# Regrouping the attention matmuls of the second block by head, with the 16 meta keys in 16-row and 16-column tiles

## The chip, the cores and the metric

The kernel runs on one core of one Trainium2 chip. The metric is the device time of one execution in microseconds. The kernel before takes 3297.89 us, the median of three runs (3297.15 to 3299.16).

## The reference

Two blocks of two layers each follow one another. The first (`hybrid_layer`: differential and stick-breaking attention over 256 tokens, model width 2048) is not touched by the change. The second puts 16 meta tokens ahead of the 256 tokens and runs two layers that mix a convolution, a recurrence and this attention, with 16 query heads of size 64, 4 key heads, a window of 128 and one sink logit per head:

```
s_meta = einsum("bnqkgd,bmkd->bkgnqm", qb, km) * scale      # 16 meta keys
s_band = einsum("bnqkgd,bnjkd->bkgnqj", qb, k_band) * scale # own and previous block of 128
probs = softmax(concatenate([s_meta, where(valid, s_band, NEG_INF), sink_col], -1))
out_r = einsum(p_meta, vm) + einsum(p_band, v_band)
s_mm = where(causal, einsum("bqkgd,bmkd->bkgqm", qmg, km) * scale, NEG_INF)  # meta queries
```

The meta queries' own outputs are needed in the first of the two layers only, since the last layer's meta rows are dropped.

## The kernel before

Weights stream from memory in halves of 128x1024 words through a ring of four buffers `raw`. ScalarE rounds each to `w_hi`, VectorE writes the rest to `w_lo`, and TensorE makes three products per tile (hi by hi, lo by hi, hi by lo). In the second block these are lines L1808 to L1810, over all 272 tokens in layer 0 and over 256 in layer 1 (`FROM[l]` is 0, then 16).

Attention is slipped in between these weight halves. Each engine's program calls `after(l, g)` behind weight half g. Heads come in eight pairs c = 0 to 7, one pair every seven halves: at the first half TensorE makes `values` of pair c-1 and `scores` of pair c, at the fourth VectorE masks (`mask_scores`), ScalarE makes the exponentials and later normalises (L829), at the fifth TensorE turns the probabilities (`turn_p`), and ScalarE copies them to `PT` and `PTm`. These instructions are in plain fp32, and each fp32 matmul that is no transpose stands in the trace as two weight loads and two matmuls.

The two heads of a pair (a = 0, 1) use two halves of the array. In `scores`, head a has its 64 features on partitions 64a to 64a+63 of `Qr` and `K2`, and writes bank 1+a of `work`. In `values`, head a writes partitions 64a to 64a+63 of bank 0. The helper `pair` (L1838 in `scores`, L1871 in `values`) issues one product for a = 0 and at once the same product for a = 1, then the next product.

Score columns are ordered meta queries' scores (`SMETA`, 16), second block (`S1`, 272), first block (`S0`, 144). The meta queries' scores take all 128 rows of Qr as stationary columns although only 16 rows matter. In `turn_p` every transpose is 128 by 128, where only 16 of the 128 rows of the three `meta` ones are used. `PTm` has 128 rows and meets a `V2[:, 2, :]` whose rows 16 and up were cleared by a memset on GpSimd (L522), the last of five steps counted by the semaphore `set2`, on which VectorE waits before it starts the second block's first row sums (L1208).

Of the kernel before, what the change touches and what calls it, by code (L numbers as in the profile page):

```python
# [28 lines left out]
ACT = mybir.ActivationFunctionType  # L29
ALU = mybir.AluOpType  # L30
AX = mybir.AxisListType

P = 128
# [11 lines left out]
MASK = -1e30  # L45
# [14 lines left out]
META = 16  # L60
TOK = META + SEQ
HD = 64
# [22 lines left out]
FROM = [0] * (DEPTH - 1) + [META]  # L85
# [3 lines left out]
E_COS = P  # L89
E_SIN = E_COS + TOK  # L90
E_MASK = E_SIN + TOK
SMETA, S1, S0, S_COLS = 0, META, META + TOK, META + TOK + META + P
E_COLS = E_MASK + S_COLS

R2_DW = 0
# [56 lines left out]
def build_program(nc, weights, x_in, consts1, params1, kept1, rope1, meta_in, ln_in, consts2, params2,  # L152
                  mats2, out):
    with ExitStack() as ctx:
        mem = Memory(nc, ctx)
# [7 lines left out]
        work = mem.psum("work", [P, 4, 512])  # L163
# [88 lines left out]
        cst2 = mem.place("cst2", [P, E_COLS])  # L252
        mat2 = mem.place("mat2", [P, M_COLS])
        par2 = mem.place("par2", [P, R2_COLS])
        SS = mem.place("SS", [P, 2, S_COLS])
        PT = mem.place("PT", [P, 2, 384])
        PTm = mem.place("PTm", [P, 2, TOK])
        Qr = mem.place("Qr", [P, TOK])
        V2 = mem.place("V2", [P, 3, 256])
        rs2 = mem.place("rs2", [P, TOK])  # L260
# [76 lines left out]

        def score_parts(l):

            return ((S1, S0), (S0, S_COLS)) + (() if FROM[l] else ((SMETA, S1),))  # L340

        def masking(l, c):

            parts = len(score_parts(l))
            each = [1, parts, 1, 1, 1, 1]
            count = sum(8 * (len(score_parts(m)) + 5) for m in range(l)) + sum(each) * c
            return list(itertools.accumulate(each, initial=count))[1:]

        def exps_made(l, c):
# [61 lines left out]
        def _(pool):  # L413
# [105 lines left out]
            pool.wait_ge(set2, 2)  # L519
            pool.memset(half2, -0.5).then_inc(set2, 1)  # L520
            pool.memset(small2[:, 2:3], 1.0).then_inc(set2, 1)
            pool.memset(V2[:, 2, :], 0.0).then_inc(set2, 1)  # L522
            pool.wait_ge(set2, 5)

            pool.wait_ge(in_ss, 3)
            scale(var_in, ss_in, 1.0 / D, LN_EPS, ALU.mult, ALU.add).then_inc(in_var, 1)
# [59 lines left out]
        def _(act):  # L586
# [227 lines left out]

            def exps(l, c):
                act.wait_ge(attending, masking(l, c)[2])
                for q, (lo, hi) in enumerate(score_parts(l)):
                    for a in range(2):
                        x, i = SS[:, a, lo:hi], 2 * q + a
                        act.activation(x, x, ACT.Exp, bias=neg_m2[:, i:i + 1], accum_out=sum2[:, i:i + 1]).then_inc(a_exp, 1)  # L820
                act.wait_ge(attending, masking(l, c)[3])
                act.activation(esink, dsink, ACT.Exp).then_inc(a_exp, 1)

            def normalise(l, c):
                act.wait_ge(attending, masking(l, c)[5])
                for q, (lo, hi) in enumerate(score_parts(l)):
                    for a in range(2):
                        x, i = SS[:, a, lo:hi], 2 * q + a
                        act.activation(x, x, ACT.Copy, scale=rec2[:, i:i + 1]).then_inc(normed, 1)  # L829

            def copy_pt(l, c):
                act.wait_ge(p_turned, 8 * l + c + 1)
                act.activation(PT[:, :, :], work[:, 1:3, 0:384], ACT.Copy).then_inc(pt_copied, 1)
                for a in range(2):
                    act.activation(PTm[:, a, FROM[l]:TOK], work[:, 3 * a, FROM[l]:TOK], ACT.Copy).then_inc(pt_copied, 1)

            def copy_o(l, c):

# [24 lines left out]
            def after(l, g):  # L863
                k = FROM[l]
# [12 lines left out]
                if g == 18:  # L877
                    act.wait_ge(v2_turned, l + 1)
                    act.activation(V2[:, 0:2, :], work[:, 0, :].rearrange("p (t n) -> p t n", t=2), ACT.Copy).then_inc(v2_copied, 1)
                    act.wait_ge(set2, 5)  # L880
                    act.activation(V2[0:META, 2, :], work[0:META, 1, 0:256], ACT.Copy).then_inc(v2_copied, 1)
                c, at = divmod(g - ATT_START, ATT_STEP)
                if at == 5 and 1 <= c < 9:
# [73 lines left out]
            for l in range(DEPTH):  # L957
# [12 lines left out]
                    split2(n + 2)  # L970
                square(l, 14)

                act.wait_ge(set2, 5)
# [23 lines left out]
        def _(dve):  # L997
# [202 lines left out]

            dve.wait_ge(x_added, 4 * DEPTH)
            dve.wait_ge(set2, 5)
            groups = [(X[:, n, :], P) for n in range(NT)] + [(meta_rows[:, :], META)]
            for n, (src, r) in enumerate(groups):
                if n == 2:
# [54 lines left out]
            def mask_scores(l, c):  # L1261
                n = 8 * l + c + 1
                masks, maxima, bounds = masking(l, c)[:3]
                parts = score_parts(l)
                dve.wait_ge(scored2, n)
                first = parts[2][0] if len(parts) == 3 else S1
                mask = cst2[:, E_MASK + first:E_MASK + S_COLS].unsqueeze(1).to_broadcast([P, 2, S_COLS - first])
                dve.scalar_tensor_tensor(SS[:, :, first:S_COLS], work[:, 1:3, first:S_COLS], HD ** -0.5, mask, ALU.mult, ALU.add)\
                    .then_inc(attending, 1)
                dve.wait_ge(attending, masks)  # L1270
                for q, (lo, hi) in enumerate(parts):
                    dve.tensor_reduce(neg_m2[:, 2 * q:2 * q + 2], SS[:, :, lo:hi], AX.X, ALU.max, negate=True).then_inc(attending, 1)
# [273 lines left out]
        def _(pe):  # L1546
# [282 lines left out]
            def scores(l, c):  # L1829
                pe.wait_ge(q_ready, 3 * (8 * l + c + 1))  # L1830
                if c == 0:
                    pe.wait_ge(k2_ready, 4 * (l + 1))
                    pe.wait_ge(v2_copied, 2 * (l + 1))

                def pair(lo, hi, queries, keys, start):
                    for a in range(2):
                        half = slice(HD * a, HD * a + HD)
                        ins = pe.matmul(work[:, 1 + a, lo:hi], Qr[half, queries:queries + P], K2[half, c // 4, 0:keys], start=start,  # L1838
                                        stop=True, skip_group_check=True)
                    return ins  # L1840

                pair(S1, S0, META + P, TOK, True)
                ins = pair(S0, S_COLS, META, META + P, False)
                if FROM[l] == 0:
                    ins = pair(SMETA, S1, 0, META, False)
                ins.then_inc(scored2, 1)

            def turn_p(l, c):
                n = 8 * l + c
                pe.wait_ge(normed, scaled(l, c))  # L1850

                pe.wait_ge(o_copied, n)
                for a in range(2):
                    s, main, meta = SS[:, a, :], work[:, 1 + a, :], work[:, 3 * a, :]
                    if FROM[l] == 0:
                        pe.transpose(meta[:, 0:P], s[:, SMETA:SMETA + P], ident2)
                    pe.transpose(meta[:, META:META + P], s[:, S0:S0 + P], ident2)
                    pe.transpose(meta[:, META + P:TOK], s[:, S1:S1 + P], ident2)
                    pe.transpose(main[:, 0:P], s[:, S0 + META:S_COLS], ident2)
                    pe.transpose(main[:, P:2 * P], s[:, S1 + META:S1 + META + P], ident2)  # L1860
                    ins = pe.transpose(main[:, 2 * P:3 * P], s[:, S1 + META + P:S0], ident2)
                ins.then_inc(p_turned, 1)

            def values(l, c):
                n = 8 * l + c + 1
                pe.wait_ge(pt_copied, 3 * n)

                def pair(lo, part, p, start, stop):
                    for a in range(2):
                        v = HD * (2 * (c // 4) + a)  # L1870
                        ins = pe.matmul(work[HD * a:HD * a + HD, 0, lo:TOK], V2[:, part, v:v + HD], p[:, a, :], start=start, stop=stop,  # L1871
                                        skip_group_check=True)
                    return ins

                pair(FROM[l], 2, PTm[:, :, FROM[l]:TOK], True, False)
                pair(META, 0, PT[:, :, 0:256], False, False)
                ins = pair(META + P, 1, PT[:, :, 256:384], False, True)
                ins.then_inc(o_ready, 1)

            def lru_gate(l, n):  # L1880
# [225 lines left out]
def stack2_consts():  # L2106
# [13 lines left out]
    m = np.zeros((P, S_COLS), np.float32)  # L2120
    key = np.arange(SEQ)
    back = P + i[:, None] - key[None, :]
    m[:, S1 + META:S0] = np.where((back >= 0) & (back < P), 0.0, MASK)
    m[:, S0 + META:S_COLS] = np.where(i[None, :] <= i[:, None], 0.0, MASK)
    m[:META, SMETA:S1] = np.where(i[None, :META] <= i[:META, None], 0.0, MASK)
    c[:, E_MASK:E_MASK + S_COLS] = m
    return c

# [59 lines left out]
```

## Time and profile before

| | |
|---|---|
| runs, median | 3297.89 us |
| profiled execution, its own time | 3299.16 us |
| its span | 3297.4 us |
| TensorE matmul busy | 3236.8 us, 98% |
| VectorE busy | 1962.6 us, 60% |
| ScalarE busy | 1644.2 us, 50% |
| mean granted TensorE clock | 0.991 of full speed |
| chain that ended last | 95% TensorE |

In the trace PE is a matmul and PEld a weight load. The start of a matmul is recorded, its end is modelled, so what a matmul costs is read from the start of one to the start of the next. A form 64\*128 means that 64 rows and 128 columns of the array are used, and 64x272 the operand that streams through it. In a timeline, neighbouring instructions of one line and engine are merged into one row with their count.

### The profile page before, as it was taken

The page shows a single profiled execution, that of the slowest core. Times are in us where ns is not written, and L with a number is a line of the kernel's source. Part 1 is how long each engine was busy: PE and PEld are TensorE (multiplying, and loading weights), DVE is VectorE, ACT ScalarE, POOL GpSimd, SP SyncE. Part 2 cuts the span into 40 slices and gives each one's busy share as a digit, 9 for nine tenths or more (in the row PEclk, how much of TensorE's full clock was granted, in tenths as well). Part 3 has the DMA queues.
Part 4 walks back from the last instruction along what each step waited for, and adds up shares of the span by engine and source line. Part 5 has one row for each costly group of instructions (what it writes and reads, how often), then busy time and mean ns, then how long its engine had stood idle before and what let it go on. Part 6 is the DMA issues. An engine that isn't in the chain of part 4 may idle for free.

```text
span 3297.4 us, 48068 instructions
## 1 busy us (share of the span) xinstructions
PE 3236.8 (98%) x17416; PEld 2792.9 (85%) x17416; DVE 1962.6 (60%) x2184; ACT 1644.2 (50%) x2274; POOL 499.9 (15%) x426
## 2 busy tenths in 40 slices
PE   8999999999999999999999999999988999999998
PEld 7888888888888888888888888888868999989997
DVE  5666654444444555766645545444556887568965
ACT  5445545555444445444455555444434565355743
POOL 4544500000000003554400000000002000010000
PEclk9999999999999999999999999999998999999998
DMA  6555555545555555555554554665544444444443
GB/s 229 176 173 179 172 173 173 169 167 174 188 194 194 186 199 173 184 175 169 180 177 159 173 177 160 199 195 192 185 155 155 147 144 139 163 169 150 148 160 103
DMA packets 157147, 566.90 MB, mean 172 GB/s; under 512 B 17536, under 2 KB 19728, under 8 KB 156752
## 3 DMA queue, kind: packets, MB, share of 16 engines
q1 hardware_dynamic: 155680, 558.00, 51.6%
q0 software_dynamic: 1344, 7.16, 0.6%
q8 instruction: 89, 1.46, 0.2%
q14 instruction: 34, 0.28, 0.0%
HBM read 562.99 MB, written 2.10 MB: 171 GB/s over the span
## 4 chain that ended last, share of the span: by engine, by line
PE 95%; DVE 2%; POOL 1%; ACT 1%; issue 0%; DMA 0%; SPq 0%; POOLq 0%; ACTq 0%; DVEq 0%
PE acc L1557 22%; PE acc L1559 22%; PE acc L1558 22%; PE acc L1808 6%; PE acc L1810 6%; PE acc L1809 6%; PE work L1617 1%; PE work L1643 1%; PE work L1787 1%; PE work L1871 1%; DVE w_lo L1004 1%; PE work L1788 1%; PE work L1789 1%; PE work L1899 0%; PE work L1628 0%
## 5 line engine op out<-in xcount | busy, mean ns | idle before, releaser
L1004 DVE TENSOR_TENSOR w_lo<-raw,w_hi 128x1024 fp32r<-128x1024 f32 x1056 | 1399.1, 1334 | 1118.1 <-ACT w_hi L600 945.8
L600 ACT ACTIVATE w_hi<-raw 128x1024 fp32r<-128x1024 f32 x832 | 876.5, 1058 | 962.6 <-PE acc L1559 961.8
L1557 PE MATMUL acc<-w_hi,hT_hi 128*128 128x512 f32 x2560 | 1015.3, 397 | 2.0 <-DVE hT_lo L1010 2.0
L1559 PE MATMUL acc<-w_hi,hT_lo 128*128 128x512 f32 x2560 | 999.1, 390 | 0.0
L1558 PE MATMUL acc<-w_lo,hT_hi 128*128 128x512 f32 x2560 | 997.5, 390 | 0.0
L1559 PEld LDWEIGHTS acc<-w_hi,hT_lo 128*128 128x128 f32 x2560 | 481.1, 188 | 102.8
L1557 PEld LDWEIGHTS acc<-w_hi,hT_hi 128*128 128x128 f32 x2560 | 481.5, 188 | 97.1 <-issue 2.4
L1558 PEld LDWEIGHTS acc<-w_lo,hT_hi 128*128 128x128 f32 x2560 | 481.9, 188 | 96.0
L614 ACT ACTIVATE w_hi<-raw 128x1024 fp32r<-128x1024 f32 x224 | 236.1, 1056 | 308.2 <-PE acc L1810 295.6
L1808 PE MATMUL acc<-h_hi,w_hi 128*128 128x272 f32 (+1 forms) x1152 | 336.5, 292 | 0.0
L1810 PE MATMUL acc<-h_hi,w_lo 128*128 128x272 f32 (+1 forms) x1152 | 329.9, 286 | 0.0
L1809 PE MATMUL acc<-h_lo,w_hi 128*128 128x272 f32 (+1 forms) x1152 | 329.0, 286 | 0.0
L1808 PEld LDWEIGHTS acc<-h_hi,w_hi 128*128 128x128 f32 x1152 | 217.0, 188 | 2.0
L1809 PEld LDWEIGHTS acc<-h_lo,w_hi 128*128 128x128 f32 x1152 | 217.0, 188 | 0.8
L1810 PEld LDWEIGHTS acc<-h_hi,w_lo 128*128 128x128 f32 x1152 | 217.0, 188 | 0.0
L1557 PE MATMUL acc<-w_hi,uaT_hi 128*128 128x512 f32 x512 | 199.9, 391 | 0.0
L1559 PE MATMUL acc<-w_hi,uaT_lo 128*128 128x512 f32 x512 | 199.3, 389 | 0.0
L1558 PE MATMUL acc<-w_lo,uaT_hi 128*128 128x512 f32 x512 | 199.2, 389 | 0.0
L1808 PE MATMUL acc<-PJr,w_hi 128*128 128x272 f32 (+1 forms) x512 | 148.1, 289 | 0.0
L1810 PE MATMUL acc<-PJr,w_lo 128*128 128x272 f32 (+1 forms) x512 | 146.1, 285 | 0.0
L1809 PE MATMUL acc<-PJr,w_hi 128*128 128x272 f32 (+1 forms) x512 | 145.7, 285 | 0.0
L423 POOL TENSOR_SCALAR ZG<-TZ 128x512 f32<-128x512 f32 x32 | 34.6, 1082 | 720.2 <-ACT TZ L659 720.2
(303 smaller groups left out, 3618.0 us busy)
## 6 DMA issues: line engine op xcount, KB each, us to landing
raw<-weights SPq DMA_DIRECT2D x1056, 512.0 KB, 3.4
mat<-mats POOLq DMA_DIRECT2D x2, 1536.0 KB, 7.7
X<-x_in SPq DMA_DIRECT2D x8, 256.0 KB, 7.2
out<-out_rows SPq DMA_DIRECT2D x8, 256.0 KB, 2.5
par<-params POOLq DMA_DIRECT2D x2, 640.0 KB, 5.0
cst<-consts POOLq DMA_DIRECT2D x1, 704.0 KB, 4.9
cst<-consts POOLq DMA_DIRECT2D x1, 552.0 KB, 4.6
ropeC<-rope POOLq DMA_DIRECT2D x2, 256.0 KB, 5.2
```

The costliest lines, as they stand in the source:

```text
L423: return pool.tensor_scalar(*operands)
L600: act.activation(w_hi[:, slot, :], raw[:, slot, :], ACT.Copy).then_inc(hi_ready, 1)
L614: act.activation(w_hi[:, slot, :], raw[:, slot, :], ACT.Copy).then_inc(hi_ready, 1)
L1004: dve.tensor_tensor(w_lo[:, s % RING, :], raw[:, s % RING, :], w_hi[:, s % RING, :], ALU.subtract)\
L1557: pe.matmul(o, stat[0][:, kc, token], hi, start=(kc == 0), stop=False)
L1558: pe.matmul(o, stat[0][:, kc, token], lo, start=False, stop=False)
L1559: ins = pe.matmul(o, stat[1][:, kc, token], hi, start=False, stop=(kc == KC - 1))
L1617: ins = pe.transpose(work[:, a // 2, o:o + P], src[:, t, a, :], ident)
L1643: pe.matmul(work[:, 2 + a, 0:384], cst[:, C_NEGTRI:C_NEGTRI + P], SM[:, a, :], start=False, stop=True, skip_group_check=True)
L1808: pe.matmul(o, hi, x_hi, start=(kc == 0), stop=False)
L1809: pe.matmul(o, hi, x_lo, start=False, stop=False)
L1810: ins = pe.matmul(o, lo, x_hi, start=False, stop=(kc == KC - 1))
```

## The change

Matmuls of one head now stand together: in `scores` and in `values` the loop over a is the outer one. The meta parts become narrow: the meta queries' scores have 16 stationary columns and write 16 rows, their transpose is 16 by 16, the other two `meta` transposes take 16 columns in place of 128, and the products of `PTm` with `V2` contract over 16 rows. For that the meta queries' scores move to the end of the score columns, VectorE's mask becomes two instructions in layer 0, ScalarE's and VectorE's steps on the meta parts use 16 partitions, and the memset of `V2` goes.

```diff
-SMETA, S1, S0, S_COLS = 0, META, META + TOK, META + TOK + META + P
+S1, S0, SMETA, S_COLS = 0, TOK, TOK + META + P, TOK + META + P + META
...
-        PTm = mem.place("PTm", [P, 2, TOK])
+        PTm = mem.place("PTm", [META, 2, TOK])
...
-            return ((S1, S0), (S0, S_COLS)) + (() if FROM[l] else ((SMETA, S1),))
+            return ((P, S1, S0), (P, S0, SMETA)) + (() if FROM[l] else ((META, SMETA, S_COLS),))
...
-            pool.memset(V2[:, 2, :], 0.0).then_inc(set2, 1)
-            pool.wait_ge(set2, 5)
+            pool.wait_ge(set2, 4)
...
-            dve.wait_ge(set2, 5)
+            dve.wait_ge(set2, 4)
...
-                dve.scalar_tensor_tensor(SS[:, :, first:S_COLS], work[:, 1:3, first:S_COLS], HD ** -0.5, mask, ALU.mult, ALU.add)\
+                dve.scalar_tensor_tensor(SS[:, :, 0:SMETA], work[:, 1:3, 0:SMETA], HD ** -0.5, mask, ALU.mult, ALU.add)\
                     .then_inc(attending, 1)
+                if len(parts) == 3:
+                    mask = cst2[0:META, E_MASK + SMETA:E_MASK + S_COLS].unsqueeze(1).to_broadcast([META, 2, META])
+                    dve.scalar_tensor_tensor(SS[0:META, :, SMETA:S_COLS], work[0:META, 1:3, SMETA:S_COLS], HD ** -0.5, mask,
+                                             ALU.mult, ALU.add).then_inc(attending, 1)
...
-                pair(S1, S0, META + P, TOK, True)
-                ins = pair(S0, S_COLS, META, META + P, False)
-                if FROM[l] == 0:
-                    ins = pair(SMETA, S1, 0, META, False)
+                for a in range(2):
+                    half = slice(HD * a, HD * a + HD)
+                    k = K2[half, c // 4, :]
+                    o = work[:, 1 + a, :]
+                    pe.matmul(o[:, S1:S0], Qr[half, META + P:TOK], k, start=True, stop=True, skip_group_check=True)
+                    ins = pe.matmul(o[:, S0:SMETA], Qr[half, META:META + P], k[:, 0:META + P], start=False, stop=True,
+                                    skip_group_check=True)
+                    if FROM[l] == 0:
+                        ins = pe.matmul(o[0:META, SMETA:S_COLS], Qr[half, 0:META], k[:, 0:META], start=False, stop=True,
+                                        skip_group_check=True)
...
+                    pe.transpose(meta[0:META, META:META + P], s[:, S0:S0 + META], ident2)
                     if FROM[l] == 0:
-                        pe.transpose(meta[:, 0:P], s[:, SMETA:SMETA + P], ident2)
-                    pe.transpose(meta[:, META:META + P], s[:, S0:S0 + P], ident2)
-                    pe.transpose(meta[:, META + P:TOK], s[:, S1:S1 + P], ident2)
+                        pe.transpose(meta[0:META, 0:META], s[0:META, SMETA:S_COLS], ident2[0:META, 0:META])
+                    pe.transpose(meta[0:META, META + P:TOK], s[:, 0:META], ident2)
...
-                pair(FROM[l], 2, PTm[:, :, FROM[l]:TOK], True, False)
-                pair(META, 0, PT[:, :, 0:256], False, False)
-                ins = pair(META + P, 1, PT[:, :, 256:384], False, True)
+                for a in range(2):
+                    v = slice(HD * (2 * (c // 4) + a), HD * (2 * (c // 4) + a) + HD)
+                    o = work[HD * a:HD * a + HD, 0, :]
+                    k = FROM[l]
+                    pe.matmul(o[:, k:TOK], V2[0:META, 2, v], PTm[:, a, k:TOK], start=True, stop=False, skip_group_check=True)
+                    pe.matmul(o[:, META:TOK], V2[:, 0, v], PT[:, a, 0:256], start=False, stop=False, skip_group_check=True)
+                    ins = pe.matmul(o[:, META + P:TOK], V2[:, 1, v], PT[:, a, 256:384], start=False, stop=True, skip_group_check=True)
```

On TensorE, at the start of a head pair in layer 0 (values of the pair before, then scores of this one), these stood in a row before; x2 is the same product for a = 0 and a = 1:

```order
L1810 MATMUL acc<-h_hi,w_lo 128x272
L1871 MATMUL work<-PTm,V_96 64x272 x2
L1871 MATMUL work<-PT,V_96 64x256 x2
L1871 MATMUL work<-PT,V_96 64x128 x2
L1838 MATMUL work<-K_102,Qr 128x272 x2
L1838 MATMUL work<-K_102,Qr 128x144 x2
L1838 MATMUL work<-K_102,Qr 128x16 x2
L1808 MATMUL acc<-h_hi,w_hi 128x272
```

At the same place of TensorE's program now (the line numbers are those of the changed file):

```order
L1812 MATMUL acc<-h_hi,w_lo 128x272
L1871 MATMUL work<-PTm,V_96 64x272
L1872 MATMUL work<-PT,V_96 64x256
L1873 MATMUL work<-PT,V_96 64x128
L1871 MATMUL work<-PTm,V_96 64x272
L1872 MATMUL work<-PT,V_96 64x256
L1873 MATMUL work<-PT,V_96 64x128
L1840 MATMUL work<-K_102,Qr 128x272
L1841 MATMUL work<-K_102,Qr 128x144
L1844 MATMUL work<-K_102,Qr 16x16
L1840 MATMUL work<-K_102,Qr 128x272
L1841 MATMUL work<-K_102,Qr 128x144
```

The number of matmuls is the same; the first three of each group are head 0's, the next three head 1's (the last row, a second L1844, is cut). The L1871 ones use 16 rows of the array now, between neighbours with 128.

In `turn_p` of layer 0, TensorE turned the probabilities of one head like this before:

```order
L1856 MATMUL work<-cst_89,SS 128x128
L1857 MATMUL work<-cst_89,SS 128x128
L1858 MATMUL work<-cst_89,SS 128x128
L1859 MATMUL work<-cst_89,SS 128x128
L1860 MATMUL work<-cst_89,SS 128x128
L1861 MATMUL work<-cst_89,SS 128x128
```

Now one head has these there:

```order
L1855 MATMUL work<-cst_89,SS 16x128
L1857 MATMUL work<-cst_89,SS 16x16
L1858 MATMUL work<-cst_89,SS 16x128
L1859 MATMUL work<-cst_89,SS 128x128
L1860 MATMUL work<-cst_89,SS 128x128
L1861 MATMUL work<-cst_89,SS 128x128
```

The 16x16 one (layer 0 only) is the only one that reads 16 partitions; it has moved from the first to the second place.

## Rows read from the trace of the kernel before

**Rows 1.** Who TensorE waited for, whole span (total us, times, longest).
```profile
PE acc L1771 <- DVE meta_rows L1217: 23.7, 1, 23.7
PE acc L1993 <- ACT F L985: 12.1, 4, 6.7
PE work L1787 <- DVE h_lo L1494: 7.6, 1, 7.6
```

**Rows 2.** One pair's period, layer 0: busy PE, PEld, DVE, ACT, POOL; clock; DMA.
```profile
2544.69:2569.67 24.98, 24.98 (x204) 24.73 (x203) 17.77 (x28) 14.96 (x34) 3.10 (x3) 1.00 0.53 170
```

**Rows 3.** Timeline of scores, layer 0, pair 0: start, us, instruction.
```profile
2547.48 0.29 PE L1809 MATMUL acc<-h_lo,w_hi 128*128 128x272 f32 x1
2547.60 0.29 PE L1810 MATMUL acc<-h_hi,w_lo 128*128 128x272 f32 x1
2547.82 1.00 PEld L1838 LDWEIGHTS work<-K,Qr 64*128 64x128 f32 x12 [0.15 <-issue]
2548.85 0.19 PEld L1808 LDWEIGHTS acc<-h_hi,w_hi 128*128 128x128 f32 x1
```

**Rows 4.** Stretch at that start, line L1838 alone: PE busy (x), PEld busy (x).
```profile
2547.82:2547.83 0.01, 0.01 (x2) 0.01 (x2) 1.00 0.00 0
```

**Rows 5.** Timeline of full-array fp32 matmuls, layer 0, then layer 1.
```profile
2776.39 7.50 PE L1899 MATMUL work<-PJ,mat 128*128 128x272 f32 x32
3167.67 7.07 PE L1899 MATMUL work<-PJ,mat 128*128 128x256 f32 x32
```

**Rows 6.** Groups by form, of that line: count, busy us, mean ns.
```profile
L1899 PE MATMUL work<-PJ,mat 128*128 128x272 f32 x32 | 7.5, 392 | 0.0
L1899 PE MATMUL work<-PJ,mat 128*128 128x256 f32 x32 | 7.1, 379 | 0.0
```

**Rows 7.** Timeline of scores, layer 1, pair 0.
```profile
2950.08 0.76 PEld L1838 LDWEIGHTS work<-K,Qr 64*128 64x128 f32 x8 [0.15 <-issue]
2950.98 0.19 PEld L1808 LDWEIGHTS acc<-h_hi,w_hi 128*128 128x128 f32 x1
```

**Rows 8.** Timeline of weight loads in values, layer 0.
```profile
2596.49 0.20 PEld L1871 LDWEIGHTS work<-PTm,V 128*64 128x64 f32 x4
2596.77 0.81 PEld L1871 LDWEIGHTS work<-PT,V 128*64 128x64 f32 x8
2597.75 1.00 PEld L1838 LDWEIGHTS work<-K,Qr 64*128 64x128 f32 x12 [0.17 <-issue]
```

**Rows 9.** Timeline of weight loads in values, layer 1.
```profile
2997.26 0.20 PEld L1871 LDWEIGHTS work<-PTm,V 128*64 128x64 f32 x4
2998.49 0.30 PEld L1838 LDWEIGHTS work<-K,Qr 64*128 64x128 f32 x4 [0.17 <-issue]
```

**Rows 10.** Timeline around a 16-row transpose between full ones.
```profile
2494.84 0.29 PE L1789 MATMUL work<-h_hi,w_lo 128*128 128x272 f32 x1
2495.06 0.23 PE L1771 MATMUL acc<-cst,meta_rows 16*128 16x16 f32 x1
2495.22 0.44 PE L1774 MATMUL acc<-cst,X 128*128 128x128 f32 x2
2495.41 0.37 PE L1787 MATMUL work<-h_hi,w_hi 128*128 128x272 f32 x1
```

**Rows 11.** Timeline around a 16-column transpose.
```profile
2537.87 0.29 PE L1810 MATMUL acc<-h_hi,w_lo 128*128 128x272 f32 x1
2537.88 0.09 PEld L1823 LDWEIGHTS work<-cst,PJ 128*16 128x16 f32 x1
2537.99 0.27 PE L1823 MATMUL work<-cst,PJ 128*16 128x128 f32 x1
...
2538.10 0.38 PE L1826 MATMUL work<-cst,PJ 128*128 128x128 f32 x2
...
2538.32 0.27 PE L1823 MATMUL work<-cst,PJ 128*16 128x128 f32 x1
...
2538.43 0.38 PE L1826 MATMUL work<-cst,PJ 128*128 128x128 f32 x2
...
2538.57 0.37 PE L1808 MATMUL acc<-h_hi,w_hi 128*128 128x272 f32 x1
```

**Rows 12.** Timeline, normalising (ACT) and the turn that waits for it, layer 1.
```profile
3110.23 1.12 ACT L829 ACTIVATE SS<-SS,small 128x272 f32<-128x272 f32 x3
3111.96 0.14 PEld L1857 LDWEIGHTS work<-cst,SS 128*128 128x128 f32 x1
```

**Rows 13.** Timeline, start of the second block: GpSimd's memsets, VectorE's first sum.
```profile
2461.99 0.10 POOL L521 MEMSET small<- 128x1 f32 x1
2462.03 0.31 POOL L522 MEMSET V<- 128x256 f32 x1
2462.45 4.48 DVE L1208 TENSOR_REDUCE small<-X 128x1 f32<-128x2048 f32 x2 [2.95 <-POOL V L522]
```

**Rows 14.** Timeline of VectorE in the mask step, layer 0.
```profile
2550.22 1.05 DVE L1268 SCALAR_TENSOR_TENSOR SS<-work,cst 128x864 f32<-128x864 f32 x1
...
2552.51 0.17 DVE L1278 TENSOR_TENSOR small<-small 128x6 f32<-128x6 f32 x1
```

More of the change, by code:

```diff
@@ L338, in score_parts @@
         def score_parts(l):
-            return ((S1, S0), (S0, S_COLS)) + (() if FROM[l] else ((SMETA, S1),))
+            return ((P, S1, S0), (P, S0, SMETA)) + (() if FROM[l] else ((META, SMETA, S_COLS),))
         def masking(l, c):
             parts = len(score_parts(l))
-            each = [1, parts, 1, 1, 1, 1]
-            count = sum(8 * (len(score_parts(m)) + 5) for m in range(l)) + sum(each) * c
+            each = [max(1, parts - 1), parts, 1, 1, 1, 1]
+            count = sum(8 * (max(1, len(score_parts(m)) - 1) + len(score_parts(m)) + 4) for m in range(l)) + sum(each) * c
             return list(itertools.accumulate(each, initial=count))[1:]
@@ L816, in exps @@
                 act.wait_ge(attending, masking(l, c)[2])
-                for q, (lo, hi) in enumerate(score_parts(l)):
+                for q, (rows_n, lo, hi) in enumerate(score_parts(l)):
                     for a in range(2):
-                        x, i = SS[:, a, lo:hi], 2 * q + a
-                        act.activation(x, x, ACT.Exp, bias=neg_m2[:, i:i + 1], accum_out=sum2[:, i:i + 1]).then_inc(a_exp, 1)
+                        x, i = SS[0:rows_n, a, lo:hi], 2 * q + a
+                        act.activation(x, x, ACT.Exp, bias=neg_m2[0:rows_n, i:i + 1], accum_out=sum2[0:rows_n, i:i + 1])\
+                            .then_inc(a_exp, 1)
                 act.wait_ge(attending, masking(l, c)[3])
@@ L825, in normalise @@
                 act.wait_ge(attending, masking(l, c)[5])
-                for q, (lo, hi) in enumerate(score_parts(l)):
+                for q, (rows_n, lo, hi) in enumerate(score_parts(l)):
                     for a in range(2):
-                        x, i = SS[:, a, lo:hi], 2 * q + a
-                        act.activation(x, x, ACT.Copy, scale=rec2[:, i:i + 1]).then_inc(normed, 1)
+                        x, i = SS[0:rows_n, a, lo:hi], 2 * q + a
+                        act.activation(x, x, ACT.Copy, scale=rec2[0:rows_n, i:i + 1]).then_inc(normed, 1)
             def copy_pt(l, c):
@@ L834, in copy_pt @@
                 for a in range(2):
-                    act.activation(PTm[:, a, FROM[l]:TOK], work[:, 3 * a, FROM[l]:TOK], ACT.Copy).then_inc(pt_copied, 1)
+                    act.activation(PTm[:, a, FROM[l]:TOK], work[0:META, 3 * a, FROM[l]:TOK], ACT.Copy).then_inc(pt_copied, 1)
             def copy_o(l, c):
@@ L879, in after @@
                     act.activation(V2[:, 0:2, :], work[:, 0, :].rearrange("p (t n) -> p t n", t=2), ACT.Copy).then_inc(v2_copied, 1)
-                    act.wait_ge(set2, 5)
                     act.activation(V2[0:META, 2, :], work[0:META, 1, 0:256], ACT.Copy).then_inc(v2_copied, 1)
@@ L971, in _ @@
                 square(l, 14)
-                act.wait_ge(set2, 5)
+                act.wait_ge(set2, 4)
                 act.activation(small2[:, 1:2], small2[:, 2:3], ACT.Sqrt)
@@ L1265, in mask_scores @@
                 dve.wait_ge(scored2, n)
-                first = parts[2][0] if len(parts) == 3 else S1
-                mask = cst2[:, E_MASK + first:E_MASK + S_COLS].unsqueeze(1).to_broadcast([P, 2, S_COLS - first])
-                dve.scalar_tensor_tensor(SS[:, :, first:S_COLS], work[:, 1:3, first:S_COLS], HD ** -0.5, mask, ALU.mult, ALU.add)\
+                mask = cst2[:, E_MASK:E_MASK + SMETA].unsqueeze(1).to_broadcast([P, 2, SMETA])
+                dve.scalar_tensor_tensor(SS[:, :, 0:SMETA], work[:, 1:3, 0:SMETA], HD ** -0.5, mask, ALU.mult, ALU.add)\
                     .then_inc(attending, 1)
+                if len(parts) == 3:
+                    mask = cst2[0:META, E_MASK + SMETA:E_MASK + S_COLS].unsqueeze(1).to_broadcast([META, 2, META])
+                    dve.scalar_tensor_tensor(SS[0:META, :, SMETA:S_COLS], work[0:META, 1:3, SMETA:S_COLS], HD ** -0.5, mask,
+                                             ALU.mult, ALU.add).then_inc(attending, 1)
                 dve.wait_ge(attending, masks)
-                for q, (lo, hi) in enumerate(parts):
-                    dve.tensor_reduce(neg_m2[:, 2 * q:2 * q + 2], SS[:, :, lo:hi], AX.X, ALU.max, negate=True).then_inc(attending, 1)
+                for q, (r, lo, hi) in enumerate(parts):
+                    dve.tensor_reduce(neg_m2[0:r, 2 * q:2 * q + 2], SS[0:r, :, lo:hi], AX.X, ALU.max, negate=True).then_inc(attending, 1)
                 dve.wait_ge(attending, maxima)
@@ L1833, in scores @@
                     pe.wait_ge(v2_copied, 2 * (l + 1))
[L1835 to L1840, printed above, removed]
-                pair(S1, S0, META + P, TOK, True)
-                ins = pair(S0, S_COLS, META, META + P, False)
-                if FROM[l] == 0:
-                    ins = pair(SMETA, S1, 0, META, False)
+                for a in range(2):
[8 more added lines that the diff above has]
+                                        skip_group_check=True)
                 ins.then_inc(scored2, 1)
@@ L1854, in turn_p @@
                     s, main, meta = SS[:, a, :], work[:, 1 + a, :], work[:, 3 * a, :]
+                    pe.transpose(meta[0:META, META:META + P], s[:, S0:S0 + META], ident2)
                     if FROM[l] == 0:
-                        pe.transpose(meta[:, 0:P], s[:, SMETA:SMETA + P], ident2)
-                    pe.transpose(meta[:, META:META + P], s[:, S0:S0 + P], ident2)
-                    pe.transpose(meta[:, META + P:TOK], s[:, S1:S1 + P], ident2)
-                    pe.transpose(main[:, 0:P], s[:, S0 + META:S_COLS], ident2)
-                    pe.transpose(main[:, P:2 * P], s[:, S1 + META:S1 + META + P], ident2)
-                    ins = pe.transpose(main[:, 2 * P:3 * P], s[:, S1 + META + P:S0], ident2)
+                        pe.transpose(meta[0:META, 0:META], s[0:META, SMETA:S_COLS], ident2[0:META, 0:META])
+                    pe.transpose(meta[0:META, META + P:TOK], s[:, 0:META], ident2)
+                    pe.transpose(main[:, 0:P], s[:, S0 + META:SMETA], ident2)
+                    pe.transpose(main[:, P:2 * P], s[:, META:META + P], ident2)
+                    ins = pe.transpose(main[:, 2 * P:3 * P], s[:, META + P:TOK], ident2)
                 ins.then_inc(p_turned, 1)
@@ L1866, in values @@
                 pe.wait_ge(pt_copied, 3 * n)
[L1868 to L1873, printed above, removed]
-                pair(FROM[l], 2, PTm[:, :, FROM[l]:TOK], True, False)
-                pair(META, 0, PT[:, :, 0:256], False, False)
-                ins = pair(META + P, 1, PT[:, :, 256:384], False, True)
+                for a in range(2):
[5 more added lines that the diff above has]
+                    ins = pe.matmul(o[:, META + P:TOK], V2[:, 1, v], PT[:, a, 256:384], start=False, stop=True, skip_group_check=True)
                 ins.then_inc(o_ready, 1)
@@ L2122, in stack2_consts @@
     back = P + i[:, None] - key[None, :]
-    m[:, S1 + META:S0] = np.where((back >= 0) & (back < P), 0.0, MASK)
-    m[:, S0 + META:S_COLS] = np.where(i[None, :] <= i[:, None], 0.0, MASK)
-    m[:META, SMETA:S1] = np.where(i[None, :META] <= i[:META, None], 0.0, MASK)
+    m[:, META:TOK] = np.where((back >= 0) & (back < P), 0.0, MASK)
+    m[:, TOK + META:TOK + META + P] = np.where(i[None, :] <= i[:, None], 0.0, MASK)
+    m[:META, SMETA:S_COLS] = np.where(i[None, :META] <= i[:META, None], 0.0, MASK)
     c[:, E_MASK:E_MASK + S_COLS] = m
```

## The prediction

> **What bounds the kernel now.** I read the list of waits first. TensorE's three longest waits, 43 us together, are the change from the first block to the second, the output at the very end, and the change between the layers [rows 1]; no line of scores, values or turn is in the list. Then the busy time by stretches: in one period of a head pair (24.98 us of layer 0) TensorE is busy for all of it at full clock, VectorE for 17.77 us and ScalarE for 14.96 us [rows 2]. So in the stages that the change touches TensorE sets the time. Whatever is added to its own stream lengthens the kernel one for one, and what is taken from VectorE or ScalarE there is worth nothing. Last I read the timeline start to start inside the three attention blocks, since the change lives there: scores, turn, values, 16 times each.
>
> **Five prices from the rows.** (1) A full-array fp32 matmul record of 272 columns: 32 of them take 7.50 us, and the last one's own modelled length of 0.39 is in it, so start to start is (7.50 - 0.39)/31 = 0.229 us. For 256 columns (7.07 - 0.38)/31 = 0.216 us [rows 5, 6]. Between these a column costs about 0.85 ns; so 144 columns 0.122, 128 columns 0.109, 16 columns about 0.013 us. (2) Change of the array's shape, D: from the last weight matmul to the first load of scores is 2547.60 to 2547.82 = 0.22 us, where the weight matmul alone needs 0.126 (2547.48 to 2547.60 and their like). So D = 0.095 us. The same stands ahead of the 16-row transpose, 2494.84 to 2495.06 [rows 3, 10]. (3) Exposed load, L: the scores block of layer 1 lasts 0.90 us [rows 7], and one head's four records are 2 x 0.229 + 2 x 0.122 = 0.702; less D that leaves L = 0.107. The block of layer 0 lasts 1.03 us [rows 3]: 0.107 + 0.702 + 0.013 + a second load of 0.107 that the 16 columns can't cover + D = 1.02, which fits. (4) For values with 64 stationary columns: 1.26 us in layer 0 [rows 8] = L' + 2 x 0.229 + 2 x 0.216 + 2 x 0.109 + D, so L' = 0.056; layer 1 gives 1.23 the same way [rows 9]. (5) Six transposes stand between two weight matmuls at 2537.87 and 2538.57, two of them with 16 stationary columns: 0.70 us = 0.127 before the first, 5 x 0.109, and 0.03 after the last. So a transpose is 0.109, with 128 or 16 stationary columns alike [rows 11].
>
> The point of (3) and (4): each block lasts as long as the records of **one** head, though it holds those of two. Right at the start of scores two loads and two matmuls are in flight in the same hundredth of a microsecond [rows 4]. One after another the twelve records of scores would need 4 x (0.229 + 0.122 + 0.013) = 1.46 us, more than the 1.03 measured. The two heads run side by side on the two halves of the array.
>
> **The change part by part.**
>
> Order by head. Head 0's matmuls use one half and each must wait for the one before; head 1's first stands behind all of them. I take it that matmuls start in program order, so the second head starts when the first one's last has started, and nearly all of the overlap is gone. On top, the new shapes (16 columns in scores, 16 rows in values) stand between the others, and each change of shape costs D and an exposed load.
>
> Scores, layer 0: for each head L + 0.702 + D = 0.904, then the two 16-column records with small loads, about 0.04, and D again: 1.04. Two heads 2.08, before 1.03: +1.05 us. Scores, layer 1 (no 16-column part, one shape throughout): a second 0.702 us; the second head's load and first matmul may lie beside the first one's last record, 0.122, but its load starts only behind the first head's last load. Between 0.58 and 0.81, I take 0.68.
>
> Values, layer 0: each head L' + 0.458 + D, then L' + 0.650 + D, together 1.41; two heads 2.82, before 1.26: +1.56 us. Layer 1: 2 x (0.056 + 0.432 + 0.095 + 0.056 + 0.650 + 0.095) = 2.77, before 1.23: +1.54 us.
>
> Turn: the two transposes with 16 stationary columns save nothing, since the 128 columns of the identity stream through as before; [rows 11] show 0.109 and no wait on either side. The 16 by 16 one uses 16 rows. The nearest thing in the trace is L1771, one ahead of two full transposes: 2494.84 to 2495.41 is 0.57 us [rows 10], where two transposes alone would take 0.127 + 0.109 + 0.03 = 0.26. So it costs 0.31. Its load has 128 columns; such a load lasts 0.14 us [rows 12] against 0.09 with 16 [rows 11], so 0.05 less here, 0.26. It replaces one of 0.109: +0.15 us, for 2 heads x 8 pairs in layer 0. Its bounds are -0.08 (it costs only a short record and no shape change) and +0.20.
>
> The sum on TensorE: 8 x (1.05 + 0.68 + 1.56 + 1.54) = 38.6, and 16 x 0.15 = 2.4, together 41.0 us.
>
> Start of the second block: TensorE stands still for 23.7 us there and waits for a chain of VectorE, ScalarE and GpSimd that begins with L1208, and L1208 waits for the memset that goes. The step before it ends at 2462.09 against 2462.34 [rows 13]: -0.25 us, all on the path. If the sum's start has another cause close behind, it is 0.
>
> VectorE and ScalarE: one more mask instruction per pair in layer 0, 16 partitions by 32 elements; its bounds are the small VectorE ones of 0.17 us and the mask itself with 1.05, and 0.2 is the nearer [rows 14], the rest has the same column counts on fewer partitions; I cost the fewer partitions at nothing either way. The work lies between scores and turn. The tightest place in layer 1 has normalising end at 3111.35 and the turn's load start at 3111.96, 0.6 us of slack, and layer 1 gets no new instruction; the other pairs and layer 0 have more, and a TensorE that is 2 to 3 us slower per period widens all of them [rows 2, 12]. If that cover were gone, it would cost 0.2 x 8 = 1.6 us, and 8 us by the upper bound. The split of the weights gains the same slack, and no DMA is moved.
>
> Total +41.0 - 0.3 = **+40.7 us**. The profiled execution took 3299.16 us around a span of 3297.4 and would become 3339.9; it lies 1.3 above the median. On the median: 3297.9 + 40.7 = **3338.6 us**, 1.2% slower.
>
> The Trainium skill, TensorEngine Tiling (Array Packing), "Key Properties", states that changing the tiling mode drains TensorE while changing the tile alone does not. The 0.22 in place of 0.126 us agrees [rows 3], and between heads of one shape there is nothing of it. Read strictly it covers every change of shape that this edit adds, which is my sum; the 16-column transposes [rows 11] are a change of shape that costs nothing, so the rule is not without exception here.
>
> **The rivals.**
>
> Serial, but shape changes between small shapes are free (as for the 16-column transpose [rows 11]; against it stand the 64-row, 64-column and 16-row cases [rows 3, 8, 10]). Then 16 x 3 x (0.095 + 0.056) = 7.2 us of values, 8 x 0.4 = 3.2 of scores and 16 x 0.23 = 3.7 of the turn go: 41 - 14 = +27, **3324.6 us**.
>
> Not slower: the overlap survives the new order. The place is the start of head 1 in scores and values; if a matmul on a free half of the array may start ahead of those that queue for the busy half, the blocks stay one head long. Then only savings are left: 8 x 0.094 for the second load of the 16-column records, 16 x 0.08 in the turn, 0.25 at the start: -2.3, **3295.6 us**, no change that can be seen. It decides from the point where head 1's first matmul starts less than a record behind head 0's first. For it: two heads do run at once [rows 4]. Against: before, program order and overlap never disagree, so no row shows an overtaking.
> The same page of the Trainium skill says under "Key Properties" that different tiles can load and multiply in parallel, without a word on order; taken so, it gives this rival. TensorE: Matmul & The Clock Gate, "The mechanism", says that only loads are pulled ahead and matmuls stay in order, which gives my forecast. No row here decides between them.
>
> Slower still: the attention chain of VectorE and ScalarE becomes late, and the turn waits for it, say 1 us a pair: 3338.6 + 16 = **3355 us**. Against it: the slack above, and that TensorE slows while they don't.
>
> **How the numbers follow.** Forecast (serial, shape changes paid) 0.73, serial without them 0.17, overlap survives 0.05, late chain 0.05. The forecast's own range: the change adds 104 shape changes (48 in values, 24 in scores, 32 in the turn); 0.05 us more on each is +5, and half of them cheaper is -8, so 3331 to 3344. To take in the serial rival I go down to 3321 and up to 3346. About 0.2% (6.6 us) is what a measurement of this kernel can tell from no change. Faster by that 0.02, the same 0.04, slower 0.94.
>
> **What would show it.** In the new profile: scores blocks (first load to the next weight load) of 2.1 us in layer 0 and 1.6 in layer 1, values 2.8 us in both; two matmuls of the line in flight at a block's start reduced to one; turn 0.3 us longer per pair in layer 0 and unchanged in layer 1; L1208 0.25 us earlier against the end of the first block; TensorE without a wait in the attention. If scores and values last as before, the order does not matter and I am wrong altogether; if values last about 2.3 us, the shape changes are free.

## The result, and the profile after

The changed kernel takes 3332.32 us (median of 4 runs, 3331.73 to 3332.38) against 3298.34 us before, measured beside it: +34.0 us, ratio 1.0103 (95% interval 1.009 to 1.0116). The forecast was +40.7 us, 3338.6 us, in a range of 3321 to 3346.

The totals of the profiled execution after (span 3331.8 us), engine busy time and instruction counts:

```profile
PE 3271.6 (98%) x17416; PEld 2803.9 (84%) x17416; DVE 1960.1 (59%) x2192; ACT 1646.5 (49%) x2274; POOL 500.6 (15%) x425
```

The number of PE records is the same as before, and their busy time is 34.8 us more. VectorE and ScalarE are within 2.5 us of what they had. The longest waits of TensorE are still the three outside the attention; the first is half a microsecond shorter than in [rows 1] (the line numbers are those of the changed file):

```profile
PE acc L1773 <- DVE meta_rows L1216: 23.2, 1, 23.2
PE acc L1989 <- ACT F L984: 12.1, 4, 6.7
PE work L1789 <- DVE h_lo L1496: 7.6, 1, 7.6
```

Now the blocks. This is the timeline of weight loads of the changed kernel for one pair of layer 0, values and then scores (start, length, instruction, idle time before it):

```profile
2601.41 0.19 PEld L1871 LDWEIGHTS work<-PTm,V 16*64 16x64 f32 x2 [0.15 <-issue]
2602.01 0.19 PEld L1872 LDWEIGHTS work<-PT,V 128*64 128x64 f32 x2 [0.41 <-issue]
2602.28 0.35 PEld L1873 LDWEIGHTS work<-PT,V 128*64 128x64 f32 x2
2602.80 0.19 PEld L1871 LDWEIGHTS work<-PTm,V 16*64 16x64 f32 x2 [0.17 <-issue]
2603.40 0.19 PEld L1872 LDWEIGHTS work<-PT,V 128*64 128x64 f32 x2 [0.41 <-issue]
...
2604.20 0.29 PEld L1840 LDWEIGHTS work<-K,Qr 64*128 64x128 f32 x2 [0.17 <-issue]
2604.53 0.42 PEld L1841 LDWEIGHTS work<-K,Qr 64*128 64x128 f32 x2
2605.09 0.11 PEld L1844 LDWEIGHTS work<-K,Qr 64*16 64x16 f32 x2
2605.24 0.29 PEld L1840 LDWEIGHTS work<-K,Qr 64*128 64x128 f32 x2
...
2606.27 0.19 PEld L1810 LDWEIGHTS acc<-h_hi,w_hi 128*128 128x128 f32 x1
```

Values run from 2601.41 to 2604.20 = 2.78 us against 1.26 in [rows 8], scores from there to 2606.27 = 2.08 against 1.03 in [rows 3] (lengths are taken from times not yet rounded to the hundredth). The second head's L1871 starts 1.39 us behind the first one's, as long as a whole head. Each row that starts a new form (16\*64, 128\*64, 64\*16, 64\*128) has idle time of the weight loads before it, or stands later than the loads before it end.

Scores of layer 1, where every product has one shape, look otherwise in the same kernel:

```profile
2972.87 0.31 PEld L1840 LDWEIGHTS work<-K,Qr 64*128 64x128 f32 x4 [0.15 <-issue]
...
2973.20 0.43 PEld L1841 LDWEIGHTS work<-K,Qr 64*128 64x128 f32 x4
2973.78 0.19 PEld L1810 LDWEIGHTS acc<-h_hi,w_hi 128*128 128x128 f32 x1
```

The block lasts 0.91 us, against 0.90 in [rows 7]. Program order is L1840, L1841 of head 0 and then L1840, L1841 of head 1, yet the four loads of L1840, two of each head, come first. The busy counts in three hundredths of a microsecond (matmuls, then loads, in flight; the last stretch is in layer 0) tell when the second head joins:

```profile
2972.87:2972.88 0.01, 0.01 (x1) 0.01 (x1) 0.00 (x0) 1.00 0.00 0
2972.89:2972.90 0.01, 0.01 (x2) 0.01 (x2) 0.00 (x0) 1.00 0.00 0
2548.73:2548.74 0.01, 0.01 (x1) 0.01 (x1) 0.00 (x0) 1.00 0.00 0
```

In layer 1 it is there 0.02 us after the start (in [rows 4] in the first hundredth), although the second matmul of the first head comes only 0.33 us after its first. In layer 0 only one is in flight. So a head's matmuls do start ahead of queued ones of the other head. That is the rival that I gave 0.05, true in one place (scores of layer 1) and not in three (scores of layer 0, values of both layers).

The turn of layer 0 in the changed kernel, PE and PEld:

```profile
2566.03 0.27 PE L1855 MATMUL work<-cst,SS 128*16 128x128 f32 x1
2566.23 0.08 PEld L1857 LDWEIGHTS work<-cst,SS 16*16 16x16 f32 x1 [0.22 <-issue]
2566.24 0.18 PE L1857 MATMUL work<-cst,SS 16*16 16x16 f32 x1
...
2566.34 0.28 PE L1858 MATMUL work<-cst,SS 128*16 128x128 f32 x1
...
2566.46 0.27 PE L1859 MATMUL work<-cst,SS 128*128 128x128 f32 x1
```

From L1855 to L1859 it takes 0.43 us, and three full transposes would take 0.33 [rows 11]: the 16 by 16 one costs 0.10 more than the full one it replaces. The block of two heads is 1.51 us, before 1.32.

### The profile page after: what moved, and what is told of

Its sections match the earlier page's. It is cut to its first block, busy times and chain, and to the rows that moved or that the text cites. A ratio compares the mean times of both kernels' runs of the same rounds, so it can differ in the third digit from the quotient of the medians.

```text
span 3331.8 us, 48075 instructions
## 1 busy us (share of the span) xinstructions
PE 3271.6 (98%) x17416; PEld 2803.9 (84%) x17416; DVE 1960.1 (59%) x2192; ACT 1646.5 (49%) x2274; POOL 500.6 (15%) x425
## 4 chain that ended last, share of the span: by engine, by line
PE 95%; POOL 2%; DVE 1%; ACT 1%; issue 1%; DMA 0%; SPq 0%; POOLq 0%; ACTq 0%; DVEq 0%
PE acc L1559 22%; PE acc L1561 22%; PE acc L1560 22%; PE acc L1810 6%; PE acc L1812 6%; PE acc L1811 6%; PE work L1619 1%; PE work L1645 1%; PE work L1871 1%; PE work L1872 1%; PE work L1789 1%; PE work L1790 1%; PE work L1791 1%; PE work L1840 0%; POOL QN L465 0%
## 5 line engine op out<-in xcount | busy, mean ns | idle before, releaser
L423 POOL TENSOR_SCALAR ZG<-TZ 128x512 f32<-128x512 f32 x32 | 34.4, 1076 | 718.2 <-ACT TZ L658 718.2
```

The lines of the kernel that those rows point to most:

```text
L423: return pool.tensor_scalar(*operands)
```

## The experiments

Theory A: on their own, matmuls of the other head can start out of program order; what keeps the heads apart is a change of the array's shape between them. Theory B, from the prediction: program order keeps them apart.

**Order only.** The kernel before with the order by head, all sizes kept.

```diff
-                pair(S1, S0, META + P, TOK, True)
-                ins = pair(S0, S_COLS, META, META + P, False)
-                if FROM[l] == 0:
-                    ins = pair(SMETA, S1, 0, META, False)
+                for a in range(2):
+                    one(a, S1, S0, META + P, TOK, True)
+                    ins = one(a, S0, S_COLS, META, META + P, False)
+                    if FROM[l] == 0:
+                        ins = one(a, SMETA, S1, 0, META, False)
...
+                for a in range(2):
+                    one(a, FROM[l], 2, PTm[:, :, FROM[l]:TOK], True, False)
+                    one(a, META, 0, PT[:, :, 0:256], False, False)
+                    ins = one(a, META + P, 1, PT[:, :, 256:384], False, True)
```

> The kernel before with one edit: scores and values issue all products of head 0, then all of head 1; every operand keeps its full size. Theory A (the shape changes are the whole cost; matmuls on a free half of the array start ahead of queued ones): the scores blocks stay 1.03 us in layer 0 and 0.91 in layer 1, values 1.26 and 1.23, time 3298 us as before. Theory B (the prediction's step: head 1 starts only behind head 0's last matmul): scores of layer 0 1.8 us, values 2.3 us, 8 x 0.7 + 16 x 1.09 = +23 us, 3321 us.

Measured 3310.04 us, ratio 1.0037 (1.0022 to 1.0051), +12.1 us: between the two. The loads of values in layer 0, then one block of scores of layer 0:

```profile
2596.68 0.19 PEld L1869 LDWEIGHTS work<-PTm,V 128*64 128x64 f32 x2
2596.96 0.37 PEld L1869 LDWEIGHTS work<-PT,V 128*64 128x64 f32 x2
2597.19 0.19 PEld L1869 LDWEIGHTS work<-PTm,V 128*64 128x64 f32 x2
2597.40 0.87 PEld L1869 LDWEIGHTS work<-PT,V 128*64 128x64 f32 x6
2598.44 0.29 PEld L1837 LDWEIGHTS work<-K,Qr 64*128 64x128 f32 x2 [0.17 <-issue]
...
2572.40 1.57 PEld L1837 LDWEIGHTS work<-K,Qr 64*128 64x128 f32 x12 [0.17 <-issue]
2574.00 0.19 PEld L1808 LDWEIGHTS acc<-h_hi,w_hi 128*128 128x128 f32 x1
```

Values last 1.77 us and scores 1.59. The second head's PTm load starts at 2597.19, 0.51 us behind the first head's: not at once, and not behind all six of its matmul records (1.16 us). At that moment head 0's third matmul has started and its fourth load with it, so five instructions of head 0 that have not started (matmul, load, matmul, load, matmul) stand ahead; one matmul earlier it was seven. In scores of layer 1, with four matmul records a head, the block stayed 0.91 us, and both heads are in flight 0.02 us after its start at 2957.90, with six of head 0's instructions not started:

```profile
2957.92:2957.93 0.01, 0.01 (x2) 0.01 (x2) 1.00 0.00 0
```

So head 1 went with six ahead of it and waited with seven. The overtaking is real and reaches a limited way. Both theories are too simple: A misses the limit, B the overtaking.

**Depth.** The order-only kernel with each head's two products of layer-1 scores repeated, to see that limit.

```diff
                 for a in range(2):
+                    for _ in range(REPS[c] if l else 1):   # 1, 2, 3, 4, 6, 8, 10, 12
```

> The order-only kernel; in layer 1 each head's two products of scores are issued r times over before the other head's begin, with r = 1, 2, 3, 4, 6, 8, 10, 12 for the eight pairs (the repeats write the same scores again). Head 1's first weight load then stands 8r weight loads and matmuls behind head 0's. If the overlap has no limit of depth, the block lasts 0.107 + 0.702 r + 0.095 us: 0.9, 1.6, 2.3, 3.0, 4.4, 5.8, 7.2, 8.6 and the kernel 3298 + 38 x 0.702 = 3325 us. If TensorE looks only a certain way ahead, the block grows towards 0.2 + 1.40 r from some r on (17 us at r = 12), and head 1's first load moves away from head 0's.

One run, 3365.45 us. The blocks of r = 2, 8 and 12 repeats:

```profile
2983.60 2.27 PEld L1838 LDWEIGHTS work<-K,Qr 64*128 64x128 f32 x16 [0.17 <-issue]
2986.01 0.19 PEld L1809 LDWEIGHTS acc<-h_hi,w_hi 128*128 128x128 f32 x1
...
3099.77 10.71 PEld L1838 LDWEIGHTS work<-K,Qr 64*128 64x128 f32 x64 [0.17 <-issue]
3110.62 0.19 PEld L1809 LDWEIGHTS acc<-h_hi,w_hi 128*128 128x128 f32 x1
...
3170.80 16.34 PEld L1838 LDWEIGHTS work<-K,Qr 64*128 64x128 f32 x96 [0.17 <-issue]
3187.28 0.19 PEld L1809 LDWEIGHTS acc<-h_hi,w_hi 128*128 128x128 f32 x1
```

The rule "head 1's first load starts when at most six instructions that have not started stand ahead of it" means: it starts with head 0's fourth matmul from the end. From r = 2 on, with the prices of the prediction, the block is 0.107 + (r - 1) x 0.702 + 0.107 + r x 0.702 + 0.095 us: 2.41, 10.84 and 16.46 us for r = 2, 8 and 12. Measured: 2.41, 10.85 and 16.48. For r = 3, 4, 6 and 10 the same trace gives 3.82, 5.23, 8.04 and 13.67 us, where the rule gives 3.82, 5.22, 8.03 and 13.65. At r = 1 the fourth from the end is the first, the two heads start together and the block is 0.91. The expectation of an unlimited depth (1.6, 5.8, 8.6) falls.

The limit goes by the number of instructions and not by the time they take. In scores of layer 0 of the order-only kernel head 1 still waited when head 0's second matmul started, with about 0.50 us of head 0's work left (0.229 + 2 x 0.122 + 2 x 0.013, an estimate from the prices). In layer 1 it went with 0.70 us left.

**Two at a time.** The same limit, tried the other way round.

```diff
+                for a in range(2):
+                    one(a, FROM[l], 2, PTm[:, :, FROM[l]:TOK], True, False)
+                    one(a, META, 0, PT[:, :, 0:256], False, False)
+                for a in range(2):
+                    ins = one(a, META + P, 1, PT[:, :, 256:384], False, True)
```

(and scores likewise: the two wide products by head, then the third of each head.)

> The kernel before with one edit: two products of head 0, two of head 1, then the third of head 0 and of head 1, all of full size. Account from the order-only and the depth run: a weight load for the free half of the array starts when no more than six instructions that have not started stand ahead of it in the queue (with all three products of a head in a row it had to wait until head 0's third matmul record started; with two products it went at once). Then nothing is lost here: scores 1.04 us in layer 0 and 0.91 in layer 1, values 1.27 and 1.24, 3298.5 us. Rival: what counts is the length of the whole block (24 instructions of three products per head are too many, 16 are not); then the blocks are as in the order-only kernel, 1.59 and 1.77 us, 3310 us.

Measured 3297.75 us, ratio 1.0 (0.999 to 1.0009). Values and scores of layer 0:

```profile
2596.04 0.20 PEld L1870 LDWEIGHTS work<-PTm,V 128*64 128x64 f32 x4
2596.33 0.81 PEld L1870 LDWEIGHTS work<-PT,V 128*64 128x64 f32 x8
2597.31 1.01 PEld L1837 LDWEIGHTS work<-K,Qr 64*128 64x128 f32 x12 [0.17 <-issue]
2598.35 0.19 PEld L1808 LDWEIGHTS acc<-h_hi,w_hi 128*128 128x128 f32 x1
```

1.27 and 1.04 us: nothing is lost. The same 24 records (loads and matmuls) stand in the block as in the order-only kernel. So what counts is how many of head 0's instructions stand ahead of head 1's next load, not the block's length.

**Values narrow.** The order-only kernel with 16 rows in the first product of values.

```diff
+                    rows_n = META if part == 2 else P
-                    return pe.matmul(work[...], V2[:, part, v:v + HD], p[:, a, :], ...)
+                    return pe.matmul(work[...], V2[0:rows_n, part, v:v + HD], p[0:rows_n, a, :], ...)
```

> The order-only kernel with one more edit: the first product of values contracts over 16 rows in place of 128 (the other 112 are zero in V2), nothing else. Theory A: three more shape changes between the heads, and with them the two heads run one after the other: values 2.78 and 2.73 us as in the changed kernel, +24 us against before, 3322.5 us. Rival: the narrow product only adds three shape changes with their loads, 16 x 3 x 0.15 = +7 us, and the heads still overlap: 3305.5 us.

Measured 3325.39 us, ratio 1.0081 (1.0065 to 1.0098), 15.4 us above the order-only kernel. Values of layer 0:

```profile
2598.62 0.19 PEld L1870 LDWEIGHTS work<-PTm,V 16*64 16x64 f32 x2
2599.21 0.62 PEld L1870 LDWEIGHTS work<-PT,V 128*64 128x64 f32 x4 [0.41 <-issue]
2600.01 0.19 PEld L1870 LDWEIGHTS work<-PTm,V 16*64 16x64 f32 x2 [0.17 <-issue]
2600.61 0.62 PEld L1870 LDWEIGHTS work<-PT,V 128*64 128x64 f32 x4 [0.41 <-issue]
2601.40 0.29 PEld L1837 LDWEIGHTS work<-K,Qr 64*128 64x128 f32 x2 [0.17 <-issue]
```

2.78 us, the changed kernel's own value. With the shape changes the overlap that the order had left is gone too: head 1's load starts 1.39 us behind, where it was 0.51. Three changes at 0.15 us would have lengthened the block by 0.45 us, and it grew by 1.01; the other 0.56 (an estimate) is lost overlap. The rival (shape changes cost their 0.15 each and no more, 3305.5 us) falls. My expected 3322.5 us was 3 us low: I had left out what the order alone costs in scores of layer 0, 8 x 0.56 us, and with it the sum is 3327.

**Narrow together.** The changed kernel with the narrow products of both heads side by side.

```diff
-                    if FROM[l] == 0:
-                        ins = pe.matmul(o[0:META, SMETA:S_COLS], Qr[half, 0:META], k[:, 0:META], start=False, ...)
+                if FROM[l] == 0:
+                    for a in range(2):
+                        half = slice(HD * a, HD * a + HD)
+                        ins = pe.matmul(work[0:META, 1 + a, SMETA:S_COLS], Qr[half, 0:META], K2[half, c // 4, 0:META], ...)
```

(in values, a loop over a for the 16-row product, then one for the other two.)

> The changed kernel with one edit: the narrow products of both heads stand next to each other (in values ahead of the others, in scores behind them), and within each group the order stays by head. Theory A: one extra change of shape per block in place of three, so values 0.056+0.458+0.095+0.056+0.650+0.095 = 1.41 us in layer 0 and 1.38 in layer 1, scores of layer 0 1.04 us, turn as in the changed kernel: 3298.3 + 16 x 0.15 + 1.5 - 0.3 = 3302 us. Theory B: PT products of values and the wide products of scores still run one head after the other: 16 x 0.65 + 8 x 0.7 = 16 us more, 3318 us.

Measured 3302.15 us, ratio 1.0012 (1.0002 to 1.0022), as theory A had it to 0.2 us:

```profile
2593.33 0.19 PEld L1872 LDWEIGHTS work<-PTm,V 16*64 16x64 f32 x4
2593.93 0.20 PEld L1877 LDWEIGHTS work<-PT,V 128*64 128x64 f32 x4 [0.41 <-issue]
...
2594.74 0.31 PEld L1840 LDWEIGHTS work<-K,Qr 64*128 64x128 f32 x4 [0.17 <-issue]
...
2595.65 0.11 PEld L1846 LDWEIGHTS work<-K,Qr 64*16 64x16 f32 x4
2595.80 0.19 PEld L1810 LDWEIGHTS acc<-h_hi,w_hi 128*128 128x128 f32 x1
```

Values 1.41 us, scores 1.06. All rows come in fours again, so narrow shapes do run side by side. Placed together, with one more change of shape per block and the longer turn, the narrow shapes cost 4 us over the kernel before; placed between the heads they cost 22 over the order-only kernel.

**The memset's wait.** The kernel before, with VectorE waiting for four of GpSimd's steps.

```diff
-            dve.wait_ge(set2, 5)
+            dve.wait_ge(set2, 4)
```

> The kernel before with one edit: VectorE's wait ahead of the second block's first row sums is on four steps of GpSimd in place of five, so that the memset of V2 is not waited for. The only part of the change that can shorten the path: the sums start 0.25 us earlier after the first block's end, TensorE's wait there falls from 23.7 to about 23.4 us, the time is 0.25 us less than before, which the timing cannot tell from none (3298 us). Rival: something else starts the sums; then the distance stays 4.59 us.

Measured 3297.75 us, ratio 0.9999 (0.999 to 1.0009): no change that the timing can tell, as expected. Its timeline and its first wait:

```profile
2455.77 0.39 PE L1559 MATMUL acc<-w_hi,uaT_lo 128*128 128x512 f32 x1
...
2460.12 2.29 DVE L1208 TENSOR_REDUCE small<-X 128x1 f32<-128x2048 f32 x1 [2.70 <-POOL small L521]
...
PE acc L1771 <- DVE meta_rows L1217: 23.5, 1, 23.5
```

The sums start 4.35 us behind the last matmul of the first block, and that start is released by L521 where it was L522 in [rows 13]. TensorE's wait is 23.5 for 23.7 us. The changed kernel has 23.2. Its other quarter of a microsecond lies further down the same chain: GpSimd's first step (L423) starts 0.38 us behind the start of ScalarE's last step ahead of it, where it was 0.69 in the kernel before and in this one. Why is not shown.

No version ran faster than the kernel before beyond what the timing can tell.

The blocks, in us (first load of the block to the next weight load behind it; scores and values for layer 0 / layer 1, turn for layer 0). The kernel with the memset's wait has those of the kernel before:

| kernel | scores | values | turn | time |
|---|---|---|---|---|
| before | 1.03 / 0.90 | 1.26 / 1.23 | 1.32 | 3298.3 |
| changed | 2.08 / 0.91 | 2.78 / 2.73 | 1.51 | 3332.3 |
| order only | 1.59 / 0.91 | 1.77 / 1.71 | 1.32 | 3310.0 |
| values narrow | 1.59 / 0.91 | 2.78 / 2.73 | 1.32 | 3325.4 |
| narrow together | 1.06 / 0.91 | 1.41 / 1.39 | 1.51 | 3302.2 |
| two at a time | 1.04 / 0.91 | 1.27 / 1.24 | 1.32 | 3297.8 |

## Why the prediction was right, and where not

**The bound** held. Eight times each, the blocks grew by 8 x (1.05 + 0.01 + 1.52 + 1.50 + 0.19) = 34.1 us, and the time by 34.0. With the 0.5 us shorter wait at the start of the second block, 33.6 were due; the 0.4 between is less than this timing can tell. No part of the blocks' growth was hidden, and no new wait for VectorE or ScalarE appeared.

**Scores, layer 0:** forecast +1.05, measured 1.03 to 2.08, +1.05. **Values:** forecast +1.56 and +1.54, measured +1.52 and +1.50. **Turn:** forecast +0.30 a pair, measured +0.19. I took the price from the trace's other 16-row transpose, whose successor loads 128 columns behind the shape change; here it loads 16. The successor takes 0.165 us to the next matmul there and 0.114 here, which fits the 0.05 a head that I had too much. **Start of the second block:** forecast -0.25, measured -0.5. The memset's wait gave half of it, the quarter on GpSimd the other.

**The step that failed** is "I take it that matmuls start in program order, so the second head starts when the first one's last has started". It gave +0.68 us to scores of layer 1, 5.4 us of the sum, and there it measured +0.01. The runs put this in its place: the second head's instructions start out of program order as long as no more than six unstarted ones stand ahead and no change of shape lies between. The 5.4 us are most of the 6.7 us by which the sum was too high.

The same step was half wrong where the number came out right. In layer 0 and in values I charged the loss of the overlap to the order. The order alone costs 8 x (0.56 + 0.51 + 0.48) = 12.4 us by the blocks, 12.1 us by the timing. The other 21.7 us of 34.1 come from the narrow shapes: 8 x (0.49 + 1.01 + 1.02 + 0.19), the last term in the turn and the others between the heads. The forecast had the right total for these blocks because with the shape changes in between TensorE does fall back to the program's order, the case that I computed. That I computed it without this reason was luck: the same step without shape changes gives 2.3 us for values, and the order-only kernel measured 1.77.

The rival in which shape changes are free (3324.6 us) would have shown values of about 2.3 us; they took 2.78. The late chain of VectorE and ScalarE (3355 us) would have shown TensorE waiting in the turn; its list of waits has no line of it.

The Trainium skill, TensorE: Matmul & The Clock Gate, "The mechanism", states that only loads are pulled ahead while matmuls stay in order. This trace does not agree: in layer 1 head 1's first matmul is in flight 0.02 us after head 0's first, with head 0's other three still queued. The Trainium skill, TensorEngine Tiling (Array Packing), "Key Properties", states that a change of tiling mode drains TensorE. The trace agrees in these blocks, at 0.095 us a change.

## What to carry to other kernels

Where two small matmuls share the array by halves, keep their instructions close: at this kernel's sizes two fp32 products of one half in a row are harmless and three are not. A narrower operand that gives the array another shape was no saving on TensorE: placed best, with those of both heads together, it added 0.15 us to a block of values, 0.03 to a block of scores and 0.10 to a head's turn. Between two matmuls that ran side by side it cost their overlap as well. Put the odd shapes of all halves next to each other, or pad them to the common shape.

## What the runs showed of the hardware

- A change of the array's shape takes 0.095 us and the next load, 0.107 us for 128 fp32 columns and 0.056 for 64. With one between the heads, the second head's first load came only behind all of the first head's matmuls (1.39 us in values, 0.51 without it). A transpose with 16 stationary columns between full ones costs nothing extra, although it is a change of form [rows 11].
